# Third and fourth feed-forward: from the ninth pair on, x's high and low parts pass in one 512-column matmul

## The reference, cut to what matters

```python
def swiglu(x, w1, w3, w2):            # x 256 x 1024, w1 and w3 1024 x 2816
    return (silu(x @ w1) * (x @ w3)) @ w2
x = layer_norm_2(DEEPNORM_ALPHA * x + mix, ln1_g[i], ln1_b[i])
x = layer_norm_2(DEEPNORM_ALPHA * x + swiglu(x, ffn_w1[i], ffn_w3[i], ffn_w2[i]), ln2_g[i], ln2_b[i])
```

## Time and profile before

| | |
|---|---|
| median of 3 runs | 1417.07 us (1416.36 to 1417.62) |
| the profiled execution, its own time | 1416.97 us |
| its span, first to last instruction | 1415.2 us |
| TensorE busy | 1389.9 us, 98% of the span |
| VectorE, ScalarE, GpSimd busy | 1020.8, 933.0 and 391.2 us (72%, 66%, 28%) |
| granted TensorE clock | 1.0 |
| third up-projection | about 852 to 974 us |
| fourth up-projection | about 1196 to 1318 us |

### The profile page before, as it was taken

The page is one execution under the profiler, slowest core; times in us unless marked ns, Lnnn a source line. Parts: engine busy times, 40 slices in busy tenths (PEclk is TensorE's granted clock), DMA queues, the critical chain, the costliest instruction groups (busy, mean ns, idle before and its releaser), DMA issues.

```text
span 1415.2 us, 30766 instructions
## 1 busy us (share of the span) xinstructions
PE 1389.9 (98%) x11080; PEld 1345.6 (95%) x11080; DVE 1020.8 (72%) x1653; ACT 933.0 (66%) x1569; POOL 391.2 (28%) x389
## 2 busy tenths in 40 slices
PE   9999999999999999999999999999999999999998
PEld 7899889999999999999999899999999989999998
DVE  7867766888748888887488857665478876766557
ACT  5633437655876576558867766557878787655866
POOL 4343002332303243334053224212034401421203
PEclk9999999999999999999999999999999999999999
DMA  6533215555665655666745236555655615655662
GB/s 217 177 105 102 64 37 162 169 174 177 194 194 162 180 164 164 178 177 185 206 153 187 61 105 190 181 179 171 203 160 166 208 47 152 199 186 182 188 191 93
DMA packets 62728, 226.04 MB, mean 160 GB/s; under 512 B 6960, under 2 KB 8240, under 8 KB 62640
## 3 DMA queue, kind: packets, MB, share of 16 engines
q1 hardware_dynamic: 61776, 221.87, 51.4%
q10 hardware_dynamic: 864, 3.01, 0.6%
HBM read 223.80 MB, written 1.05 MB: 159 GB/s over the span
## 4 chain that ended last, share of the span: by engine, by line
PE 68%; DVE 18%; issue 6%; ACT 5%; DMA 1%; DVEq 1%; POOL 0%; SPq 0%; ACTq 0%
PE bank L425 18%; PE bank L426 18%; PE bank L427 18%; DVE w_lo L1747 7%; DVE cv L2143 2%; PE bank L474 1%; DVE x_lo L1775 1%; ACT w_hi L1128 1%; DVE tu L1798 1%; PE bank L463 1%; PE bank L467 1%; PE bank L885 1%; PE bank L886 1%; PE bank L887 1%; DVE tg L1798 1%
## 5 line engine op out<-in xcount | busy, mean ns | idle before, releaser
L425 PE MATMUL bank<-x_hi,w_hi 128*128 128x258 f32 (+6 forms) x2096 | 600.8, 287 | 4.4 <-DVE w_lo L1747 2.0
L426 PE MATMUL bank<-x_lo,w_hi 128*128 128x258 f32 (+6 forms) x2096 | 592.9, 283 | 0.0
L427 PE MATMUL bank<-x_hi,w_lo 128*128 128x258 f32 (+6 forms) x2096 | 592.9, 283 | 0.0
L1747 DVE TENSOR_TENSOR w_lo<-raw,w_hi 128x1024 fp32r<-128x1024 f32 x295 | 374.7, 1285 | 47.3 <-ACT w_hi L1128 32.8
L425 PEld LDWEIGHTS bank<-x_hi,w_hi 128*128 128x128 f32 x2096 | 395.5, 189 | 13.1 <-issue 9.9
L1128 ACT ACTIVATE w_hi<-raw 128x1024 fp32r<-128x1024 f32 x299 | 313.3, 1053 | 131.0 <-PE bank L427 107.9
L426 PEld LDWEIGHTS bank<-x_lo,w_hi 128*128 128x128 f32 x2096 | 396.0, 189 | 0.4
L427 PEld LDWEIGHTS bank<-x_hi,w_lo 128*128 128x128 f32 x2096 | 395.8, 189 | 0.0
L1745 DVE SCALAR_TENSOR_TENSOR w_lo<-raw,negmean,w_hi 128x1024 fp32r<-128x1024 f32 x120 | 159.9, 1335 | 140.6 <-ACT w_hi L1126 139.4
L427 PE MATMUL bank<-a_hi,w_lo 128*128 (+2 forms) x704 | 198.0, 281 | 0.0
L426 PE MATMUL bank<-a_lo,w_hi 128*128 (+2 forms) x704 | 197.9, 281 | 0.0
(11 more groups left out here) (456 smaller groups left out, 2229.9 us busy)
## 6 DMA issues: line engine op xcount, KB each, us to landing
raw<-w SPq DMA_DIRECT2D x419, 512.0 KB, 3.7
h<-h SPq DMA_DIRECT2D x2, 544.0 KB, 5.7
out<-h SPq DMA_DIRECT2D x8, 128.0 KB, 1.9
T<-cs ACTq DMA_DIRECT2D x1, 960.0 KB, 5.7
con_b<-cb ACTq DMA_DIRECT2D x1, 712.0 KB, 4.5
smx<-pin ACTq DMA_DIRECT2D x1, 512.0 KB, 5.3
con_g<-ca ACTq DMA_DIRECT2D x1, 421.5 KB, 6.4
prm<-par ACTq DMA_DIRECT2D x1, 202.0 KB, 4.5
```

What stands on the lines that cost most here:

```text
L425: pe.matmul(o, wh, xh, start=first, stop=False)
L426: pe.matmul(o, wh, xl, start=False, stop=False)
L427: return pe.matmul(o, wl, xh, start=False, stop=last)
L1747: V.tensor_tensor(w_lo[:, slot, :], raw[:, slot, :], w_hi[:, slot, :].bitcast(F32), ALU.subtract).then_inc(S("lo_ready"), 1)
```

## The change

In the third and fourth up-projections the first eight pairs stay as they were. From the ninth pair on (units 16 to 43, 28 of each up-projection) the moving operand is no longer g r with its bias column but the finished normalised x, in a new tile `x2` that holds its high part and its low part side by side for each block of K. High weights pass both at once, in one matmul of 512 columns, which fills a whole bank; low weights pass the high part in 256 columns. So for each block of K there are two matmuls (512 and 256 columns) in place of three of 258. At eviction the two halves of the bank are added: ACT copies the upper half into `cv`, DVE adds the lower half to it. There is no multiplication by 1/std and no bias there.

`x2` is made during pairs 0 to 7: ACT writes the high part (one more instruction for each of the 8 tiles, two tiles in pair 0, one in each of pairs 1 to 6), DVE the low part (two tiles in pair 1, one in each of pairs 2 to 7, ahead of `tg`). POOL computes its first tile of h ahead of the loop, and each later one a pair earlier. TensorE waits for all eight low parts of `x2` before unit 16.

```diff
+RAW_PAIRS = 8
+            x2 = sb("x2", [P, 2, KT, SEQ], F32R, where=ffn)
@@ TensorE
+            def high_and_low(u0, n):
+                def body(u, s, j):
+                    slot = s % RING
+                    start_unit(u, s)
+                    for k in range(KT):
+                        c = slice(k * P, k * P + P)
+                        o = acc[slot]
+                        if k < KT - 1:
+                            pe.matmul(o[:, 0:2 * SEQ], w_hi[:, slot, c], x2[:, :, k, :], start=(k == 0), stop=False)
+                            pe.matmul(o[:, 0:SEQ], w_lo[:, slot, c], x2[:, 0, k, :], start=False, stop=False)
+                        else:
+                            pe.matmul(o[:, 0:SEQ], w_lo[:, slot, c], x2[:, 0, k, :], start=False, stop=False)
+                            mm = pe.matmul(o[:, 0:2 * SEQ], w_hi[:, slot, c], x2[:, :, k, :], start=False, stop=True)
+                    mm.then_inc(S("unit_done"), 1)
+                units(pe, u0, n, body)
+            def plain_ups(n, u0):
+                after_norm(n, u0, SEQ)
+                panels(u0 + 2, 2 * RAW_PAIRS - 2, SEQ + 2)
+                pe.wait_ge(S("x2_ready"), KT * (n // 2 - 1))
+                high_and_low(u0 + 2 * RAW_PAIRS, 36 - 2 * RAW_PAIRS)
+                mean_of_h(n + 1, SEQ)
+                high_and_low(u0 + 36, 2 * FT - 36)
+                pe.wait_ge(S("hm_set"), n + 2)
...
-                ups(n - 1, up, SEQ)
+                plain_ups(n - 1, up)
@@ ScalarE
+            def whole_pair(u, s, j):
+                par = (s - U[f"up{ups[0]}"]) // 2 % 2
+                jb = j + ups[0] * FT
+                act.wait_ge(S("unit_done"), u + 1)
+                A(cv[:, 0, 0:SEQ], acc[s % RING][:, SEQ:2 * SEQ], ACT.Copy).then_inc(S("low_half"), 1)
+                split(u + RING, s + RING)
+                row_mean(u + (RING + 1), s + RING + 1)
+                act.wait_ge(S("acc_used"), u + 1)
+                A(sl[:, par, 0:SEQ], tu[:, par, 0:SEQ], ACT.Silu).then_inc(S("ffn_silu"), 1)
+                act.wait_ge(S("unit_done"), u + 2)
+                A(cv[:, 1, 0:SEQ], acc[(s + 1) % RING][:, SEQ:2 * SEQ], ACT.Copy).then_inc(S("low_half"), 1)
+                ahead(u + 1, s + 1)
+                act.wait_ge(S("ffn_product"), jb + 1)
+                A(at(a_hi, j, slice(0, SEQ)), av[:, par, 0:SEQ], ACT.Copy).then_inc(S("a_hi"), 1)
...
-                    if isinstance(j, int) and j < KT:
+                    if conv is None:
+                        for k in ((0, 1) if j == 0 else (j + 1,) if j < KT - 1 else ()):
+                            which = (3, 5)[ups[0] - 2]
+                            act.wait_ge(S("ln_h1"), KT * which + k + 1)
+                            A(x2[:, 0, k, :], h[:, k, 0:SEQ], ACT.Identity, bias=par_col(f"ln_b{2 * ups[0]}", k), scale=par_col(f"ln_g{2 * ups[0]}", k)).then_inc(S("x2_hi"), 1)
+                            gain_and_bias(2 * ups[0], which, k, N)
+                    elif isinstance(j, int) and j < KT:
@@ VectorE
+            def whole_pair(u, s, j):
+                n = ups[0]
+                first = U[f"up{n}"] + 2 * RAW_PAIRS
+                halves = u + (2 * (FT - RAW_PAIRS) * (n - 2) - first)
+                par = (s - first) // 2 % 2
+                t, gate = tu[:, par, 0:SEQ], tg[:, par, 0:SEQ]
+                dve.wait_ge(S("low_half"), halves + 1)
+                V.tensor_tensor(t, acc[s % RING][:, 0:SEQ], cv[:, 0, 0:SEQ], ALU.add).then_inc(S("acc_used"), 1)
+                ahead(u, s)
+                ahead(u + 1, s + 1)
+                dve.wait_ge(S("low_half"), halves + 2)
+                V.tensor_tensor(gate, acc[(s + 1) % RING][:, 0:SEQ], cv[:, 1, 0:SEQ], ALU.add).then_inc(S("acc_used"), 1)
+                dve.wait_ge(S("ffn_silu"), j + (n * FT + 1))
+                dve.wait_ge(S("a_ready"), j + (n * FT + 1))
+                dve.wait_ge(S("acc_used"), u + 2)
+                V.tensor_tensor(av[:, par, 0:SEQ], gate, sl[:, par, 0:SEQ], ALU.mult).then_inc(S("ffn_product"), 1)
+                def x2_low(k):
+                    dve.wait_ge(S("x2_hi"), KT * (ups[0] - 2) + k + 1)
+                    dve.wait_ge(S("ln_h"), KT * 2 * ups[0] + k + 1)
+                    V.tensor_tensor(x2[:, 1, k, :], h[:, k, 0:SEQ], x2[:, 0, k, :].bitcast(F32), ALU.subtract).then_inc(S("x2_ready"), 1)
...
                     if not last:
                         ahead(u + 1, s + 1)
+                        if conv is None and j:
+                            for k in range(j if j > 1 else 0, j + 1):
+                                x2_low(k)
                         second_half(gate, u, s, j)
@@ GpSimd, low_parts
+                early = i >= 2
+                if early:
+                    G.tensor_tensor(h[:, 0, 0:N], r[:, 0, 0:N], rstd[:, 0:N], ALU.mult).then_inc(S("ln_h1"), 1)
                 for j in range(FT):
-                    if j < KT:
-                        G.tensor_tensor(h[:, j, 0:N], r[:, j, 0:N], rstd[:, 0:N], ALU.mult).then_inc(S("ln_h1"), 1)
+                    if j < KT - early:
+                        k = j + early
+                        G.tensor_tensor(h[:, k, 0:N], r[:, k, 0:N], rstd[:, 0:N], ALU.mult).then_inc(S("ln_h1"), 1)
```

More of the change, by code:

```diff
@@ L1354, in _ @@
             ups = [0]
+            def whole_pair(u, s, j):
[12 more added lines that the diff above has]
+                A(at(a_hi, j, slice(0, SEQ)), av[:, par, 0:SEQ], ACT.Copy).then_inc(S("a_hi"), 1)
             def up_phase(u0, N, conv):
                 base = ups[0] * FT
+                scaled = 2 * FT + RAW_PAIRS * (ups[0] - 2) if conv is None else base
                 cbase = sum(up_conv[:ups[0]]) * FT
@@ L1366, in pair @@
                     split(u + RING, s + RING)
-                    act.wait_ge(S("ffn_tu"), jb + 1)
+                    act.wait_ge(S("ffn_tu"), j + (scaled + 1))
                     if conv is not None:
@@ L1393, in up_phase @@
                     for b in range(2):
-                        pair(i * RING + (u0 + 16 + 2 * b), u0 + 16 + 2 * b, i * 2 + (8 + b))
+                        (whole_pair if conv is None else pair)(i * RING + (u0 + 16 + 2 * b), u0 + 16 + 2 * b, i * 2 + (8 + b))
                 mean_read(2 * ups[0] + 1, N)
                 for j in range(18, FT):
-                    pair(u0 + 2 * j, u0 + 2 * j, j, conv is not None and j == FT - 1)
+                    if conv is None:
+                        whole_pair(u0 + 2 * j, u0 + 2 * j, j)
+                    else:
+                        pair(u0 + 2 * j, u0 + 2 * j, j, j == FT - 1)
                 ups[0] += 1
@@ L2156, in up_phase @@
                 one_over(2 * ups[0], N)
[L2157 to L2163, removed]
+                if conv is None:
+                    for j in range(RAW_PAIRS):
+                        pair(u0 + 2 * j, u0 + 2 * j, j)
+                    with dve.Fori(0, 5) as i:
+                        for b in range(2):
+                            whole_pair(i * RING + (u0 + 16 + 2 * b), u0 + 16 + 2 * b, i * 2 + (8 + b))
+                    for j in range(18, FT):
+                        whole_pair(u0 + 2 * j, u0 + 2 * j, j)
+                else:
+                    for j in range(2):
+                        pair(u0 + 2 * j, u0 + 2 * j, j)
+                    with dve.Fori(0, 8) as i:
+                        for b in range(2):
+                            pair(i * RING + (u0 + 4 + 2 * b), u0 + 4 + 2 * b, i * 2 + (2 + b))
+                    for j in range(18, FT):
+                        pair(u0 + 2 * j, u0 + 2 * j, j, j == FT - 1)
                 ups[0] += 1
```

4 lines of the change are left out of this document (2 added, 2 removed).

## The result

| | before | after |
|---|---|---|
| median (runs) | 1417.05 us (20: 1416.36 to 1418.55) | 1418.98 us (20: 1418.22 to 1421.2) |
| ratio, 95% interval | | 1.0016 [1.0009, 1.0022] |
| profiled execution / its span | 1416.97 / 1415.2 us | 1418.46 / 1416.7 us |

The forecast was 1412.4 us, 1410.5 to 1415.0. The time lies above the range, and on the other side of no change, if by less than the 0.2% that count here as a difference.

A forecast was written before the change was run, and what follows sets the result against it. The prediction took TensorE's matmul count times start distance as the bound in the changed up-projections. From 1416.97 us it took 6.3 for shorter units and added 1.7 for two waits: 1412.4 us, range 1410.5 to 1415.0.

The forecast's parts named there:

- What bounds it: Changed up-projections: time is matmul count times start distance; a shrunk distance is won in full, a TensorE wait lost in full.
- A unit after, and what that price rests on: Units 16 to 43: 2.758 us each instead of 2.87, 6.3 us won over 56; priced from 512-column products with weights moving.
- joining wins 9.2 ns: Units 16 to 43: one 512-column matmul takes 226.8 ns, two of 256 take 236.0; 74 ns a unit.
- the gap between two runs: Large matmul reading x2: its two runs of 256 might cost like two matmuls, leaving the lower bound of 2.2 us.
- The new wait before unit 16: TensorE waits 0.75 us for x2's eighth low part, 0.85 with the slow restart; 1.7 us over two up-projections.
- Making x2, pairs 0 to 7: The added ScalarE, VectorE and GpSimd work is hidden by TensorE's matmuls: no cost, or a few tenths per up-projection.
- It has caught up by pair 5: Pairs 0 to 7: VectorE, at 4.9 us a pair against TensorE's 5.74, is back in step two pairs before it matters.
- A late VectorE would lengthen the wait one for one: Before unit 16: any VectorE lateness adds equally to TensorE's wait; bounds for both waits together 1.4 to 3.0 us.
- Whole pairs, weights: Pairs 8 to 21: added copies and additions hidden, VectorE idle 0.95 us a pair; weight stream 4% faster at no cost.
- the third rival, the ring: Whole pairs: ScalarE and VectorE depend on each other and set the pace; 1423 us at 5.9 us a pair; chance 0.06.
- the first, joining wins nothing: Units 16 to 43: only the fewer columns win, 2.2 us, against waits of 1.7; 1416.5 us, no change; chance 0.17.
- the range's upper end: 1415.0 us: the dear price of the large matmul, winning 4.4 us, with waits of 2.5 us.

The follow-up runs named there:

- e3: Changed kernel, with unit 16 taken out of the loop and waiting before each block only for that block's low part of x2: 1414.69 us, ratio 0.998.
- e5: Changed kernel making x2 but never reading it: units 16 to 43 as before the change, no wait for x2: 1417.49 us, ratio 1.0001.
- e2: Changed kernel with the 512-column matmul split into two of 256 in seven of eight blocks of K: 1420.1 us, ratio 1.0021.
- e1: Changed kernel with x2's high and low part of a block adjacent, so 512 moving columns are one run: 1418.84 us, ratio 1.0015.
- e4: Changed kernel with GpSimd making all eight tiles of h ahead of the pairs instead of one a pair: 1416.74 us, ratio 0.9997.
- e6: As e5, x2 made but not read, plus the changed kernel's TensorE wait before unit 16: 1423.29 us, ratio 1.0045.

## Why the prediction was wrong, step by step

- **What bounds it**: right. A distance that shrank was won in full, and a wait was lost in full (e3, e5).
- **A unit after, and what that price rests on**: the term that failed, by size. "I take 226.8" and "joining wins 9.2 ns" carried a price from one kind of product and one order to another. Measured: 0.235 us for the large matmul, 0.0536 us won a unit in place of 0.112, -3.0 us in place of -6.3. By e2 some 7 of the 74 ns of the joining are left, and the other 46 are the columns, forecast at 39. The doubt that I named beside it, the gap between two runs, was the wrong one (e1).
- **The new wait before unit 16**: the second term that failed, +4.5 us in place of +1.7, and by it the sign turned. The forecast of 0.75 goes to the measured 2.15 like this: TensorE was there 0.21 earlier; the first matmul came 0.33 behind the subtraction's end (894.06 to 894.39) where I had 0.08, +0.25, which is the loop's entry behind the wait, a step that the forecast did not have; and the subtraction started at 893.65, not 892.71, +0.94. Of the last, 0.48 is `tu` (890.25 against 889.77) and 0.54 the `w_lo` under `a_lo`, less 0.08 between the two.
- **Making x2, pairs 0 to 7**: the reason for it. "It has caught up by pair 5" was false. The late start was not the reason: pair 2 began 1.7 us later against TensorE (863.90), not 1.2, and at 4.9 us a pair VectorE would still have been in step by pair 7 (863.90 + 5 x 4.9 = 888.4, where TensorE lets `tu` start at about 889.6). The price of a pair was. I had the 1.72 us of GpSimd's tile of h in the earlier trace rows and called it "a place, not a time". The price of the low part, 0.44, came from rows with little or no GpSimd beside them (459 ns in the mean, 420 for `tg`), while it takes 0.95 here in each of pairs 2 to 6; VectorE and GpSimd hold each other in every one of them, and 4.9 us became 5.28. e4, which moves GpSimd's tiles of h away from these pairs, gives 4.7 and a wait of 0.8 in place of 2.0; this shows the cause. The cover of TensorE's matmuls itself held: e5 is at no change. "A late VectorE would lengthen the wait one for one" was right, and is what happened.
- **Whole pairs, weights**: hidden, as forecast. VectorE idles 1.8 to 1.9 us a pair there, ahead of `tu` (about 1 was forecast), so the third rival, the ring, did not close; the clock of the stretch stayed 1.00, with the weights at 185 GB/s.
- **The clock**: not foreseen. TensorE never stood still in the middle of these stretches before; now it does. In e1's profile the fall that followed cost 1.5 us; after's eight slower executions lie 2.1 us above the others.
- **The rivals**: the first, joining wins nothing, was nearly right about the units, but its 1416.5 kept the short waits; with the measured ones it gives 1419.3. No rival had a longer wait, though the range's upper end carried one of 2.5 us in all, not 4.5. The Trainium skill's rule ("TensorE: Matmul & The Clock Gate", "Back-to-back issue gap"), by which the units win 2.2 us, was nearer to the measured 3.0 than my price, while its level does not fit, and the page gives it for a matmul by itself, which the forecast left out.

The earlier trace rows had shown VectorE waiting 1.68 us in pair 7, and I took this slack as given at the moment of the new wait. The added work used up all of it, and `tu` came another 0.48 later.

The Trainium skill ("SBUF — State Buffer", section "SBUF: two separate sides") says that VectorE, in an operation with two SBUF inputs, and GpSimd, where it reads SBUF, take a shared pair of ports as an exclusive lock, and that the loser waits for the whole instruction. The trace agrees in order and size: h's tile, issued at 871.49, ends at 873.21, 0.60 behind the end of VectorE's two `w_lo` (872.61), not far from its own time alone of 0.74; and the subtraction issued at 872.53 ends 0.28 behind the tile.

## What to carry to other kernels

The price of an instruction is that of its place: take a VectorE subtraction of two SBUF tiles from a row with GpSimd working if GpSimd works beside it in the new place, and a matmul's distance from the same kind and order of products. A new wait in a stream that never waits should be cut to what the next instruction needs (by block: some 4 us here for a few lines), with no loop's entry between it and the matmul, because its length is the sum of all small delays ahead of it, and the idle time can cost TensorE its clock on top. The idea of the change was good: with the wait by block and the products sorted it takes 1411.3 us, 5.9 below before.

## What the runs showed of the hardware that I had not expected

- A TensorE wait of 2.0 us in the middle of a full stream was followed by some 3.4 us at 1.2 GHz in the profiles of e1 and e6, and by none in those of after and e2.
- The distance between two fp32r matmuls depends on more than their columns and neighbours: the same eight small ones take 0.91 or 0.94 us. Per column at the full clock: 0.443 to 0.461 ns for 512, 0.446 to 0.469 for 256 and 258.
- A VectorE subtraction of 128x256 takes 0.41 us alone and 0.96 with GpSimd at work, two of 128x1024 2.36 and 2.91, GpSimd's multiplication of 128x256 0.74 and, with VectorE at work, 1.72; and the overlap keeps itself going, since late VectorE work releases GpSimd work onto VectorE's next one.
